# A two-block sequence model on one core: the weights of the second block loaded earlier, its norms two tiles ahead, its convolution beside the features

## What is computed

```python
def hybrid_mixer_2(h, norm_g, w_in, ...):          # second block, all float32
    z = rms_norm_2(h, norm_g) @ w_in                # 1024 x 1792
    y_a = mixer_spatial_gating(z[:, 0:384], z[:, 384:768], ...)     # u * (W_s rms(v) + b) in blocks of 128 tokens
    y_b = mixer_rglru(z[:, 768:1152], z[:, 1152:1536], ...)         # conv of width 4, two gates, recurrence over tokens
    y_c = mixer_s5(z[:, 1536:1792], ...)                            # complex diagonal state space, gelu, GLU
    y = concat(rms_norm_2(y_a), rms_norm_2(y_b), rms_norm_2(y_c))
    return y @ w_out

h = h + mix
ffn = hierarchical_moe(rms_norm_2(h, g), router_group_w, ...)       # one of 4 groups, 2 of its 4 experts
out = rms_norm_2(h + ffn, final_norm_g)
```

## Time and profile before

| | before |
|---|---|
| median of 3 runs | 4397.45 us (4394.4 to 4401.79) |
| profiled execution | 4397.35 us, its span 4396.1 us |
| PE busy, DVE busy | 3819.4 us (87%), 1888.1 us (43%) |
| last add of the feed-forward | starts at 3152.69 us |
| first product for u and v | 3190.18 us |
| first feature product | 3351.92 us |
| first product of the route stage | 3580.09 us |
| mean granted clock of PE | 0.922 |

### The profile page before, as it was taken

How to read it: one execution, slowest core, us unless ns; L and a number is a source line. 1 busy time by engine, 2 the same in 40 slices (tenths; PEclk the granted TensorE clock), 3 DMA queues, 4 the chain that set the end, 5 groups by cost and what they waited for, 6 DMA issues and landing times.

```text
span 4396.1 us, 42115 instructions
## 1 busy us (share of the span) xinstructions
PE 3819.4 (87%) x16939; PEld 2487.4 (57%) x16939; DVE 1888.1 (43%) x3388; ACT 1005.3 (23%) x1807; POOL 692.6 (16%) x662
## 2 busy tenths in 40 slices
PE   4888798899999998888789999999688859699995
PEld 3555454577777775555454788888554535333331
DVE  5565573356566545666534343434325432200003
ACT  2333222222222213333223222222111311111111
POOL 1111000101000001111000101001010000355554
PEclk9999899899999999999799999999888979799997
DMA  5000351122222230000411111111201020587633
GB/s 183 22 22 22 127 160 65 31 67 67 72 81 77 72 123 32 22 22 17 151 62 33 39 48 48 48 45 42 84 29 43 3 90 26 227 312 279 220 101 134
DMA packets 226707, 368.71 MB, mean 84 GB/s; under 512 B 54344, under 2 KB 156226, under 8 KB 214224
## 3 DMA queue, kind: packets, MB, share of 16 engines
q1 hardware_dynamic: 168316, 230.98, 15.6%
q0 software_dynamic: 47232, 121.75, 7.8%
q10 hardware_dynamic: 10964, 13.30, 0.9%
HBM read 523.17 MB, written 44.04 MB: 129 GB/s over the span
## 4 chain that ended last, share of the span: by engine, by line
PE 80%; DVE 8%; ACT 5%; POOL 2%; issue 2%; DMA 2%; ACTq 1%; SPq 0%; DVEq 0%; POOLq 0%
PE psum L223 65%; PE psum L2885 11%; PE psum L231 3%; DVE arena L457 2%; POOL stat L638 1%; DVE arena L404 1%; DMA tmp_mixed<-arena 1%; POOL arena L3019 0%; DVE arena L1575 0%; POOL stat L268 0%; ACTq L2520 0%; ACT scratch L833 0%; DMA arena<-in_expert_w_gate,be_i 0%; ACT arena L780 0%; ACT arena L823 0%
## 5 line engine op out<-in xcount | busy, mean ns | idle before, releaser
L223 PE MATMUL psum<-arena_r,arena_r 128*128 128x512 f32 x4096 | 1336.4, 407 | 41.7 <-POOL weight_ring_r L1534 18.8
L223 PE MATMUL psum<-arena 128*128 128x128 f32 (+11 forms) x4568 | 1063.7, 413 | 179.6 <-DVE arena L966 128.7
L223 PEld LDWEIGHTS psum<-arena 128*128 128x128 f32 (+3 forms) x4568 | 637.5, 208 | 579.0 <-issue 326.4
L223 PEld LDWEIGHTS psum<-arena_r,arena_r 128*128 128x128 f32 x4096 | 793.7, 194 | 238.3 <-issue 44.0
L1575 DVE TENSOR_TENSOR arena<-arena,psum 128x512 f32<-128x512 f32 x512 | 343.2, 686 | 231.4 <-PE psum L223 231.0
L223 PE MATMUL psum<-weight_ring_r,arena_r 128*128 128x512 f32 x1024 | 423.9, 414 | 0.0
L223 PE MATMUL psum<-arena_r,weight_ring_r 128*128 128x512 f32 x1024 | 401.9, 392 | 0.0
L223 PE MATMUL psum<-arena,weight_ring 128*128 128x512 f32 x768 | 341.2, 605 | 12.2 <-ACT weight_ring L1283 7.1
L1534 POOL TENSOR_TENSOR weight_ring_r<-weight_ring,arena_r 128x2048 fp32r<-128x2048 f32 x32 | 152.1, 4754 | 1246.8 <-ACT arena_r L1499 1246.8
L2885 PE MATMUL psum<-arena 128*64 128x512 f32 x1536 | 343.5, 600 | 3.8 <-DMA arena<-in_expert_w_gate,be_i 2.3
L1566 DVE TENSOR_TENSOR arena_r<-arena,arena_r 128x512 fp32r<-128x512 f32 x128 | 88.6, 693 | 519.5 <-ACT arena_r L1527 519.5
(11 more groups left out here) (376 smaller groups left out, 3367.9 us busy)
## 6 DMA issues: line engine op xcount, KB each, us to landing
weight_ring<-in_w_mlp_up SPq DMA_DIRECT2D x32, 1024.0 KB, 6.4
weight_ring<-in_w_mlp_down SPq DMA_DIRECT2D x32, 1024.0 KB, 5.0
arena<-in_w_ada SPq DMA_DIRECT2D x24, 1024.0 KB, 6.8
arena<-in_w_ada SPq DMA_DIRECT2D x40, 512.0 KB
arena<-in_w_in SPq DMA_DIRECT2D x6, 2048.0 KB, 18.0
tmp_ys<-arena SPq DMA_DIRECT2D x24, 512.0 KB, 3.5
arena<-in_w_out SPq DMA_DIRECT2D x2, 4096.0 KB, 21.8
arena<-tmp_mixed SPq DMA_DIRECT2D x16, 512.0 KB, 3.3
```

What stands on the lines that cost most here:

```text
L223: i = self.nc.tensor.matmul(out, lhs, rhs, start=start and n == 0, stop=stop and n == len(pairs) - 1)
```

## The change

The stages and their arithmetic stay; places in memory, the issuing queue, and the order on each engine change.

- `sp_second_ahead` (new) issues the vectors, `ws`, `vg` and `w_a` from SP after the last `up` product of the feed-forward, and three of the four feature groups after the last but one `down` chunk. `sp_gating` issues the fourth and then the state space's inputs.
- x is no longer read back for the gating: norms read `k.ff.x`, the tile that the feed-forward leaves. `xn` and `u` have two buffers, the norm of tile t+2 or t+3 is made ahead, DVE writes `hT2` directly, and POOL's copy is gone.
- PE runs products of tile t, gate of t-1, put of t-2, transposes of t+2. The gate and puts of the last tiles are between the first features.
- `act_decay`, `dve_decay` (6 small instructions) are moved ahead of the state space's start and of the first feature reads. The convolution no longer waits for the last feature; `pe_recurrence` comes before `pe_ssm_weights`; the eight `w_in` copies go from ACT to DVE.
- `sp_route_ahead` (new) issues w_out in three parts and x in four, with the router's weights behind the first part of x; DVE's multiplication by the gain (`dve_route_weights`) is split over three places. The copy into `yt` is gone.

```diff
+def sp_second_ahead(k):
+    nc, S_, E, V, d = k.nc, k.S, k.sp, k.gat, k.d
+    s = nc.sync
+    E.wait_ge(S_.ff_pe.at("up", LAST, FFC - 1, 3))
+    row = 0
+    for src, n, _ in V.pieces:
+        s.dma_start(V.rows[row:row + n], src).then_inc(*S_.cols_in.dma())
+        row += n
+    s.dma_start(V.ws, d["a_spatial_w_2"][0].rearrange("h i j -> i h j")).then_inc(*S_.ws_in.dma())
+    s.dma_start(V.vg, d["a_v_norm_g_2"][0].partition_broadcast(P)).then_inc(*S_.vg_in.dma())
+    s.dma_start(V.w_a, d["w_in_2"][0].rearrange("(k p) n -> p k n", p=P)[:, :, 0:2 * AW]).then_inc(*S_.w_a_in.dma())
+    E.wait_ge(S_.ff_pe.at("down", LAST, FFC - 2, NT - 1, 1))
+    for g in (3, 0, 1):
+        sp_feature_weights(k, g)
 def sp_gating(k):
-    before_second(k, E)
+    k.sp.wait_ge(k.S.ff_pe.at("down", LAST, FFC - 1, NT - 1, 1), ff_done(k))
+    sp_feature_weights(k, 2)
     sp_ssm_inputs(k)
-    for t in range(NT):
-        if t > 0:
-            E.wait_ge(S_.gat_dve.at("xn", t - 1))
-        nc.sync.dma_start(V.xt, k.d["x_res"][at(t), :]).then_inc(*S_.x_in.dma("second", t))
...
+    for t in range(NT):
+        pe_gat_features(k, t)
+        if t >= 1:
+            pe_gat_gate(k, t - 1)
+        if t >= 2:
+            pe_gat_put(k, t - 2)
+        if t + 2 < NT:
+            pe_gat_turn(k, t + 2)
...
 def pe_features(k):
+    pe_feature(k, 0)
+    pe_gat_gate(k, NT - 1)
+    pe_gat_put(k, NT - 2)
+    pe_feature(k, 1)
+    pe_gat_put(k, NT - 1)
     pe_ssm_turn_c(k)
+    for u in range(2, 16):
+        pe_feature(k, u)
...
 def act_rt_gather(k, t):
     S_, E, V = k.S, k.act, k.rt
     if t > 0:
-        E.wait_ge(S_.rt_pe.at("seg", 6 * t - 1), S_.rt_pe.at("norms", t - 1))
-    k.nc.scalar.activation(V.yt, k.yT[:, :, at(t)], ACT.Copy).then_inc(*S_.rt_act.up("yt", t))
+        E.wait_ge(S_.rt_pe.at("norms", t - 1))
...
 def act_program(k):
     act_gating(k)
+    act_decay(k)
     act_ssm_start(k)
     act_features(k)
-    act_ssm_weights(k)
     act_recurrence(k)
...
 def pe_program(k):
     pe_features(k)
+    pe_recurrence(k)
     pe_ssm_weights(k)
     pe_ssm_in(k)
-    pe_recurrence(k)
     pe_ssm_out(k)
```

More of the change, by code:

```diff
@@ L1626, in second_views @@
     V = k.gat = Views()
-    V.w_a = A.take(KC, 2 * AW)
-    V.xt, V.xn, V.hT = A.take(D), A.take(D), A.take(KC, P)
-    V.wsT, V.ws = A.take(AH, P), A.take(AH, P)
-    V.u, V.vv, V.junk, V.ya, V.vg = A.take(AW), A.take(AW), A.take(AW), A.take(AW), A.take(AW)
-    V.rows = A.take(P)
+    V.w_a, V.ws, V.vg, V.rows = A.take(KC, 2 * AW), A.take(AH, P), A.take(AW), A.take(P)
+    V.xn, V.wsT = [A.take(D) for _ in range(2)], A.take(AH, P)
+    V.u, V.vv, V.junk, V.ya = [A.take(AW) for _ in range(2)], A.take(AW), A.take(AW), A.take(AW)
+    V.x = k.ff.x
     k.cols = k.small
@@ L1713, in pe_gat_features @@
     for n, what in enumerate("uv"):
-        if t > 0:
-            E.wait_ge(S_.gat_act.at(what, t - 1))
-        k.mm(k.ps[2 + n][:, 0:AW], [(V.hT[:, c, :], V.w_a[:, c, at(n, AW)]) for c in range(KC)]).then_inc(*S_.gat_pe.up(what, t))
+        E.wait_ge(S_.gat_act.at(what, t - 1) if t > 0 else S_.gat_dve.at("wsT"))
+        k.mm(k.ps[2 + n][:, 0:AW], [(k.hT2[:, c, at(t)], V.w_a[:, c, at(n, AW)]) for c in range(KC)]).then_inc(*S_.gat_pe.up(what, t))
 def pe_gat_gate(k, t):
@@ L1738, in pe_gating @@
     S_, E, V = k.S, k.pe, k.gat
-    before_second(k, E)
-    E.wait_ge(S_.cols_in.at())
-    k.turn([(k.ps[0][:, 0:V.n_rows], V.rows[0:V.n_rows])]).then_inc(*S_.gat_pe.up("cols"))
+    E.wait_ge(ff_done(k), S_.cols_in.at())
+    k.turn([(k.ps[5][:, 0:V.n_rows], V.rows[0:V.n_rows])]).then_inc(*S_.gat_pe.up("cols"))
+    pe_gat_turn(k, 0)
     E.wait_ge(S_.ws_in.at())
     for n in range(2):
-        k.turn([(k.ps[1 + n][:, at(j)], V.ws[:, 3 * n + j, :]) for j in range(3)]).then_inc(*S_.gat_pe.up("ws", n))
@@ L1985, in dve_features, with last_feature_read, pe_feature @@
-def dve_features(k):
+def last_feature_read(k, bank):
+    return feature_read(k, 8 + FEATURE_BANKS.index(bank))
+def pe_feature(k, u):
+    S_, E = k.S, k.pe
+    c, half = FEATURES[u // 2], u % 2
+    E.wait_ge(ff_arrived(k, feature_slot(c // 2)).at("features", c // 2))
+    if u >= 8:
+        E.wait_ge(feature_read(k, u - 8))
+    else:
+        E.wait_ge((S_.gat_dve.at("h", NT - 1, 0), S_.gat_dve.at("h", NT - 1, 1), S_.gat_act.at("u", NT - 1), S_.gat_act.at("v", NT - 1),
+                   ff_done(k), S_.gat_dve.at("sv", NT - 1), S_.gat_act.at("put", NT - 1), S_.ssm_dve.at("C"))[u])
+    w = k.ff.up_w[feature_slot(c // 2)]
+    k.mm(feature_bank(k, u), [(w[:, kc, at(c % 2)], k.hT2[:, kc, at(half, 512)]) for kc in range(KC)]).then_inc(*S_.feat_pe.up(c, half))
@@ L1990, in dve_features @@
         for half in range(2):
             E.wait_ge(S_.feat_pe.at(c, half))
-            bank = k.ps[feature_use(c, half) % 8]
+            bank = feature_bank(k, feature_use(c, half))
             if c < BC:
@@ L2401, in dve_ssm_done @@
     S_, E, V = k.S, k.dve, k.ssm
+    for t in range(6, NT):
+        E.wait_ge(x_stored(k, t).at(LAST))
     for c in range(2):
@@ L2465, in pe_route @@
     before_route(k, E)
-    E.wait_ge(S_.w_route_in.at(), S_.rt_dve.at("w"))
     pe_rt_norms(k, 0)
     pe_rt_residual(k, 0)
+    E.wait_ge(S_.w_route_in.at())
     pe_rt_norms(k, 1)
@@ L2625, in dve_route @@
     v.memset(V.cnt, 0.0).then_inc(*E.up())
-    E.wait_ge(S_.w_out_in.at("second"))
-    for c in range(KC):
-        i = v.tensor_scalar(V.w[:, c, :], V.w[:, c, :], k.cols[:, 8 + c:9 + c], None, ALU.mult)
-    i.then_inc(*S_.rt_dve.up("w"))
-    E.wait_ge(S_.x_all_in.at("second"), S_.w_route_in.at())
+    dve_route_weights(k, (7,), S_.w_out_c)
     dve_rt_norms(k, 0)
@@ L2794, in expert_views @@
     n = KC * D_EXP
-    A = Area(k.arena, 2 * KC * S)
+    A = Area(k.arena, 18432 + NT * D)
     ring = k.weights.rearrange("p a b -> p (a b)")
     V.w = {"gate": [k.arena[:, c * n:(c + 1) * n] for c in range(2)], "up": [ring[:, c * n:(c + 1) * n] for c in range(2)],
-           "down": [A.take(n) for _ in range(2)]}
+           "down": [k.arena[:, (2 + c) * n:(3 + c) * n] for c in range(2)]}
     V.xg = [A.take(D) for _ in range(2)]
@@ L2993, in combine_views @@
 def combine_views(k):
-    A, V = Area(k.arena, 2 * KC * S), Views()
-    k.comb = V
-    V.y = A.take(NT, 2, D)
-    V.junk, V.gain = A.take(D), k.scratch[:]
+    V = k.comb = Views()
+    V.y = Area(k.arena).take(NT, 2, D)
+    V.junk, V.gain = Area(k.arena, 18432 + NT * D).take(D), k.scratch[:]
 def before_combine(k, E):
```

395 lines of the change are left out of this document (200 added, 195 removed).

## The result

The changed kernel takes **4256.14 us** (median, 4249.71 to 4258.57), the kernel before 4396.48 beside it: ratio **0.9677, 95% interval 0.966 to 0.9694**, 3.2% faster. I had forecast 4275 in a range from 4256 to 4302. The profiled execution has a span of 4256.6 us; before it was 4396.1.

A forecast was written before the change was run, and what follows sets the result against it. PE bounds the kernel, kept from work from the feed-forward's last add to the route stage's end. Gains 30.8 + 56.3 - 16.0 + 39.1 + 12.8 = 123.0 off 4397.35 gave 4275 us; own range 4262 to 4288, 8-in-10 range 4256 to 4302.

The forecast's parts named there:

- term B: Gating loop, first u/v product to first feature product: PE runs without waits, 161.7 us becomes 105.4, gain 56.3.
- term E: Route stage without the copy into `yt`: idle time 7 us and clock 5.8 saved, gain 12.8, between 7 and 20.
- term D: Last feature product to first route product: 116.5 us becomes 77.4, gain 39.1, made of the convolution and ACT's issuing.
- A: Last feed-forward add to first u/v product: x on chip, `w_a` issued early, 37.5 us becomes 6.7, gain 30.8.
- C: Feature products: 111.68 us becomes 127.7, loss 16.0, with PE waiting 12.4 us for DVE's first bank read.
- The upper end: Gating loop, best case: the first tile's products are warm too, 1 us more gain.
- rival 1: PE's clock keeps falling in gating and route: costs 23 and 6 us, at most 4304, half 4290; chance 0.2.
- Router's weights late: Route stage: small transfers on SP take 40 us instead of 20, PE waits 17 us: 4292; chance 0.12.
- No wait at u = 8: Features: DVE starts sooner, PE does not wait at the ninth half, up to 12.4 + 2.5 us back: 4260; chance 0.08.
- early loads late: Loads issued early do not land in time, sharing queues with the stores of x: up to 21 us, 4296; chance 0.05.
- slower: PE's clock stays at the lower level for the whole gating and feature stages, 210 us more: 4485; chance 0.02.

The follow-up runs named there:

- gate_early: The changed kernel with PE making the gate of tile t right behind tile t's products, not behind those of t + 1: 4294.1 us, ratio to before 0.9763.
- copy_back: The changed kernel with ACT copying each tile of yT into a buffer again for PE's residual products in the route stage: 4274.8 us, ratio to before 0.9723.

## Why the prediction was right and where it was off

The prediction failed in the size of three terms of its sum, not in what bounds the kernel. The step that failed most is the length of the new gating loop, term B: 105.4 us by the sum, 98.9 measured. Behind it come the clock's share of term E (5.8 for 11.0) and `pe_ssm_in` in term D (9.35 for 7.43). A clock taken too low is in all three: it makes 2.2 of the 6.5 us in B, 5.2 of the 5.4 in E and 1.9 of the 3.0 in D.

- **What bounds.** Right: PE, in three places. Two terms came out nearly as forecast: A 31.8 for 30.8, C -15.5 for -16.0 with the wait of 12.60 for 12.4.
- **A**, by its parts: x on chip about 25, `w_a` early 6.4, and 3.0 more of `w_a` in stretch B. "If `w_a` were late by a whole landing, 21 us of it go" was wrong by half: issued late, it landed in 11.0 us, and that cost 9.
- **B was mis-sized by 6.5 us**, the largest part of the miss. The step is "12.79 + 7 x 11.94 = 96.4. Six turns at 1.09 and six puts at three eighths": I took the first tile cold, 12.79, and it took 10.56: before, PE had stood for 13.16 us ahead of that tile's transposes, and now no wait in front of it is longer than 1.02 (with one of 6.81 it takes 13.53). The upper end allowed 1 us for that, and it was 2.2. A gate and products take 11.77, not 11.94, 0.17 less in each of seven tiles, 1.2 in all. The other 3 are turns, puts and pieces that I laid end to end in the sum, while in the trace each begins 0.1 to 0.2 us before the one ahead of it ends: the period is 3221.89 - 3209.07 = 12.8, where I had 13.4. "So PE runs without waits" was exact, and rival 1, the falling clock, is false here: 1.00. That it would come back with the waits is shown by `gate_early`.
- **D was mis-sized by 3.0, and its reasons were partly wrong.** "The convolution's 14.6 us and the 29 us of ACT's issuing are what it is made of": the convolution gives 7.5. The issuing on ACT costs 1.5 by itself in this stretch, and 18.6 together with the backlog ahead of it. The sum still came near, because I had costed the new stretch from DVE's row of work and not by subtracting these two from the old. Its worst step was `pe_ssm_in` at 9.35, the row of before; it took 7.43. It also began at 18.6 us, where the sum has 19.9. From its end to the first route product it took 48.3 us, for 48.2 in the sum.
- **E was mis-sized by 5.4.** "I take somewhat under half of that as saved, 5.8": the clock gave 11.0, the idle time 7.2 (7 predicted). I had taken the clock's share as one part in doubt and cut it; `copy_back` shows that it comes back with the idle time, whole.
- **The rivals.** Router's weights late: no wait of PE for them, and issuing took 10.3 us, not 20. No wait at u = 8, early loads late, slower: none happened. Rival 1, the clock that falls without idle time, is true only of the route stage, where a tile's 16 residual products take 15.68 in some tiles and 13.98 in others.
- **The range** ended where the measurement lies, or by the ratio just short of it. It had room for the rivals, which but for one all cost time, and little for a better result: B's upper end was 1 us, and 6.5 came. All five terms came out better than forecast, none worse, so their misses added up instead of cancelling: 1.0 + 6.5 + 0.5 + 3.0 + 5.4 = 16.4, and 1.4 behind them.

## What to carry to other kernels

Waits of 1 to 3 us in PE's way cost here about one and a half to two and a half times their length, since the clock fell with them: 21 us of waits cost 35 in the gating loop, 7 cost 18 in the route stage. Price an order that removes them with the rows at full clock for every product, the first tile too. When an engine waits behind its own issuing, look at what stands in the queues ahead of the small transfers before moving them to another engine. And ahead of a wait for an engine that works through a long program, ask which of its short steps can be put sooner: four bank reads moved gave some 11 us, two products moved some 5.
